# Where the second half of w_out lands: a ninth weight buffer instead of a ring slot, in a one-core hybrid decoder step

## What is computed

```
h     = rmsnorm(x, norm_mix);  proj = h @ w_in            # 1024 x 3840
o_hg  = hgrn2_mix(proj[:HG]);  o_rw = rwkv7_mix(proj[HG:])
x     = x + concat(o_hg, o_rw) @ w_out                     # 1024 x 1024
hf    = rmsnorm(x, norm_ffn);  top-4 of 32 experts by softmax router
x     = x + sum over chosen experts: gate * (((up + 1) * glu) @ w_down[e] + b_down[e])
y     = rmsnorm(x, norm_final)
```

## Time and profile before

| | |
|---|---|
| median of 3 runs | 1215.06 us (1214.51 to 1216.84) |
| profiled execution, its own time | 1214.87 us |
| its span in the profile | 1212.8 us |
| TensorE (PE) busy | 1190.9 us, 98% |
| VectorE, ScalarE, POOL busy | 447.0, 260.7, 43.8 us |
| moved by DMA | 436.11 MB, mean 360 GB/s |

### The profile page before, as it was taken

How to read it: one execution, slowest core, us unless ns; L and a number is a source line. 1 busy time by engine, 2 the same in 40 slices (tenths; PEclk the granted TensorE clock), 3 DMA queues, 4 the chain that set the end, 5 groups by cost and what they waited for, 6 DMA issues and landing times.

```text
span 1212.8 us, 18289 instructions
## 1 busy us (share of the span) xinstructions
PE 1190.9 (98%) x7828; PEld 574.9 (47%) x7828; DVE 447.0 (37%) x967; ACT 260.7 (21%) x637; POOL 43.8 (4%) x101
## 2 busy tenths in 40 slices
PE   8999999999999999999999999999999999999996
PEld 6777777645344344434443444344444444343332
DVE  3367766754413332332233133213432323222324
ACT  3114534432221111111121211021111111111213
POOL 8000110100000000000000000000000000000000
PEclk9999999999999999999999999999999999999999
DMA  9732202499999999999999999999999999999995
GB/s 288 180 105 70 80 4 73 145 394 395 418 427 429 426 413 428 426 433 429 430 430 432 431 431 431 431 431 431 430 431 430 431 432 431 431 429 427 424 423 226
DMA packets 49388, 436.11 MB, mean 360 GB/s; under 512 B 11525, under 2 KB 26952, under 8 KB 31770
## 3 DMA queue, kind: packets, MB, share of 16 engines
q1 hardware_dynamic: 48180, 431.74, 86.3%
q0 software_dynamic: 960, 3.02, 0.8%
q10 hardware_dynamic: 166, 0.15, 0.0%
HBM read 430.01 MB, written 4.89 MB: 359 GB/s over the span
## 4 chain that ended last, share of the span: by engine, by line
PE 88%; DMA 10%; DVE 1%; ACT 1%; issue 0%; SPq 0%; DVEq 0%; ACTq 0%
PE bank L1629 32%; PE bank L1665 16%; PE bank L923 10%; PE bank L1595 8%; DMA ring<-in_w_gate_up 7%; PE bank L1699 4%; PE bank L1390 3%; DMA ring<-in_w_down 3%; PE bank L1656 3%; PE bank L1690 1%; PE bank L1142 1%; PE bank L910 1%; PE bank L956 1%; PE bank L1119 1%; PE bank L1732 0%; DMA hx<-in_state_shift 0%
## 5 line engine op out<-in xcount | busy, mean ns | idle before, releaser
L1629 PE MATMUL bank<-ring,mix 128*64 128x512 f32 x1504 | 344.5, 598 | 3.5 <-DMA ring<-in_w_gate_up 3.4
L1629 PEld LDWEIGHTS bank<-ring,mix 128*64 128x64 f32 x1504 | 101.3, 136 | 201.5 <-issue 197.3
L1665 PE MATMUL bank<-ring,mix 128*64 128x512 f32 x736 | 168.2, 598 | 0.8 <-DMA ring<-in_w_down 0.8
L2983 DVE TENSOR_TENSOR hTb<-bank,w2a 128x512 f32<-128x512 f32 x32 | 22.1, 692 | 361.8 <-PE bank L1656 361.8
L923 PE MATMUL bank<-hTb,ring 128*128 128x328 f32 (+1 forms) x416 | 121.0, 442 | 0.8 <-DVE hTb L2424 0.4
L2215 ACT ACTIVATE mix<-bank,nf 128x256 f32<-128x256 f32 x64 | 26.9, 471 | 433.0 <-PE bank L1595 433.0
L1629 PE MATMUL bank<-mix 128*64 128x512 f32 x500 | 112.7, 595 | 1.6 <-DMA mix<-in_w_gate_up 1.6
L3035 DVE TENSOR_TENSOR mix<-mix,bank 128x512 f32<-128x512 f32 x70 | 48.2, 689 | 160.0 <-PE bank L1699 144.1
L923 PEld LDWEIGHTS bank<-hTb,ring 128*128 128x128 f32 x416 | 76.7, 190 | 34.0 <-issue 2.0
L1665 PEld LDWEIGHTS bank<-ring,mix 128*64 128x64 f32 x736 | 49.3, 136 | 90.0 <-issue 84.0
L1629 PEld LDWEIGHTS bank<-mix 128*64 128x64 f32 x500 | 35.3, 137 | 71.5 <-issue 70.0
(11 more groups left out here) (448 smaller groups left out, 1096.5 us busy)
## 6 DMA issues: line engine op xcount, KB each, us to landing
ring<-in_w_gate_up SPq DMA_DIRECT2D x30, 4096.0 KB, 23.4
ring<-in_w_gate_up SPq DMA_DIRECT2D x32, 2048.0 KB, 15.6
ring<-in_w_down SPq DMA_DIRECT2D x15, 4096.0 KB, 23.8
mix<-in_w_gate_up SPq DMA_DIRECT2D x10, 4096.0 KB, 24.2
ring<-in_w_down SPq DMA_DIRECT2D x14, 2048.0 KB, 14.0
mix<-in_w_gate_up SPq DMA_DIRECT2D x11, 2048.0 KB, 14.8
mix<-in_w_down SPq DMA_DIRECT2D x5, 4096.0 KB, 25.6
ring<-in_w_in SPq DMA_DIRECT2D x14, 1024.0 KB, 5.7
```

The lines of the kernel that those rows point to most:

```text
L1629: last_ = mm(b_[64 * half:64 * half + 64, :].rearrange("s (p q) -> s p q", q=4), toks, cols[:, half], start=(c == 0), stop=(c == KT - 1))
L1665: last_ = mm(b_[r:r + 64, :], lhs, w[:, o:o + NCOL], start=(j == 0 and q == 0), stop=(j == 1 and q == 3))
```

## The change

`wo[1]` is put into the ninth buffer (`spare`) and is loaded right behind the last w_in chunk, with no wait. The three constant blocks, which lay in that buffer, go to the upper half of `gsus`. Piece 5, whose buffer in `ring` is no longer held by `wo[1]`, is loaded whole with the first group. Piece 8, the first in the ninth buffer, is now the one that comes in two halves, at the two moments that piece 5 had, and its wait for `var` 3 is gone.

```diff
-HALVES = 5
+HALVES = ONCE[0]
...
-        blk, blkm, center = (spare[:, P * i:P * i + P] for i in range(3))
...
+        blk, blkm, center = (gsus[:, NCOL + P * i:NCOL + P * i + P] for i in range(3))
...
-        wo = [at(o, 4096).rearrange("p (c n) -> p c n", n=DM) for o in (0, 8192)]
+        wo = [t.rearrange("p (c n) -> p c n", n=DM) for t in (at(0, 4096), spare[:, :])]
...
+            load(wo[1], w_out[:, 4:8, :], "x1_wo1_in")
             sync.wait_ge(S("unit_filled"), U("proj", 28))
             load(wo[0], w_out[:, 0:4, :], "x0_wo0_in")
             bg = A["b_gate_up"][0].rearrange("e (c f) -> (e c) f", c=2)
             sync.wait_ge(S("hgrn_out"), 16 * (NS + 1))
             sync.wait_ge(S("unit_filled"), U("Y0", 2))
-            load(wo[1], w_out[:, 4:8, :], "x1_wo1_in")
...
-            for k in (0, 1, PLACE["up", 1, 0], 6):
+            for k in (0, 1, PLACE["up", 1, 0], 6, 5):
                 load_piece(k)
             load(brows, bg, "nm_brow_in")
-            sync.wait_ge(S("unit_filled"), U("var", 3))
-            load_piece(ONCE[0])
             sync.wait_ge(S("mix_rw"), 3)
             load_piece(7)
```

## The result

The change made the kernel slower: 1218.62 us (median of 7 runs, 1216.73 to 1220.56) against 1215.13 us before in the same series. The ratio is 1.0026 with a 95% interval of 1.0016 to 1.0036. Measured once more beside later experiments it was 1.0021 (1.0012 to 1.0031). The forecast was 1213.9 us, no measurable change; the rival that ended on the slow side had been given 4%, and its mechanism is not the one that acted. The profiled execution shown here took 1219.97 us with a span of 1217.9 us.

The account below looks back on a forecast made before the run. The weight stream was taken to set the pace from 1001 us. -4.9 (load off the stream) + 3.8 (gap at 276 us) + 0 = -1.1 us gave 1213.9 us, no measurable change, range 1211.9 to 1215.9 us.

Parts of the forecast that it names:

- What bounds the kernel: Expert loop: the weight stream sets the pace from 1001 us; earlier stream gains one for one, up to 5.8 us.
- The early load "costs nothing": Behind the last w_in load, near 145 us: w_out's second half meets nearly idle DMA engines; 0 us.
- The gap and piece 2: Near 276 us: the queue runs dry before piece 2, so 3.8 of the 4.9 us become idle DMA time.
- p: At 276.34 us: time for piece 2's 2 MiB load to land on an empty queue, taken as 8.3 us.
- The 1.1 us live on: Stream after 276 us: later loads still find the queue busy, so the 1.1 us gain reaches the end.
- the stream's term: Weight stream: -4.9 us for the load taken off, +3.8 us for the gap at 276 us.
- Constants and halves: Three constant blocks in another buffer and piece 8 in halves instead of piece 5: 0 us.
- The sum: Whole kernel: -4.9 (load off the stream) + 3.8 (gap) + 0 (early load, constants, halves) = -1.1 us.
- The rival with the dear restart: At 276 us: piece 2 on an empty queue lands late, p say 12.0 us, making 1217.5 us; chance 4%.

Follow-up runs that it names:

- the calm version: The change with w_out's second half loaded behind an earlier w_in load, near 108 us: 1215.58 us against 1215.54 before, ratio 1.000.
- the kernel before with the extra load: The kernel before, constants moved, plus one 2 MiB load nobody reads behind the last w_in load: 1219.38 us against 1216.09, ratio 1.0030.

## Why the prediction was wrong

Its steps one by one:

- **What bounds the kernel** was not refuted: the gap of 4 us near 280 us cost nothing that can be measured. Whether an earlier stream arrives at the end one for one was not put to the test, as the stream never came out measurably earlier.
- **The early load "costs nothing"** is the step that failed. I checked it against the two things I could name there, the free share of the DMA engines (read from 188 to 196 us, not from the place of the load) and the slack of the w_in load beside it, and wrote that, were that cover gone, it would cost at most 5.9 us. I did not ask what else uses those engines. TensorE's program does: 16 KB every 4 to 5 us from 150 us on. The hint stood in the trace before: a stop of 0.24 us labelled "issue" at 152.42 us, in the middle of a group, right behind a w_in load. The measured cost is 3.45 us, 1.9 of standing still and 1.5 at half clock. With it the next assumption went, that the first half of w_out would still go at 187.07 us.
- **The gap and piece 2.** Piece 2 kept its issue (11.4 us after piece 7, as before) and landed after 7.6 us, 7.8 in the calm version. I had bounded p by 7.6 and 8.7 us and taken 8.3; it lies at the lower end. The Trainium skill's fit (DMA: Bandwidth & Descriptors, Anatomy of one DMA), by which I had estimated 6.8 us, was too low by 0.8 us for a piece and by 1.9 us for w_out.
- **"The 1.1 us live on"** was too high. The gain in landing after issue shrinks along the stream: in the calm version 9.4 - 7.8 = 1.6 us for piece 2, 9.8 - 8.5 = 1.3 us for the piece issued near 304 us, 9.7 - 9.1 = 0.6 us for the one near 319 us, and 20.8 - 20.3 = 0.5 us for the one near 467 us. From the issue of piece 7 to TensorE's last stop the calm version takes 942.2 us, the kernel before 942.7 and the kernel before with the extra load, whose stream is the same, 942.5. But the two profiles of the change take 942.5 and 942.9, and the five others with the changed stream and piece 2 whole lie between 942.3 and 942.8. So the stream's term is not told from nothing. What eats the gain between 304 and 319 us was not tried.
- **Constants and halves** cost nothing, as forecast: the calm version has both and measures 1.000.
- **The sum** should have read +3.45 for the early load and about nothing for the stream: 1218.6 us against 1215.13 before, where 1218.62 was measured and the interval of the ratio is 1.9 to 4.4 us.

The rival with the dear restart had the sign right and the place wrong; piece 2's landing was quicker than before, so nothing of it happened.
